# A seventh place for expert weights, and the expert blocks written out one by one

## The reference, cut to what matters

```python
def moe(h, w_router, b_router, w_gate, w_up, w_down):     # 16 experts, 2 for each token
    t = h.reshape(b * l, d)                               # d = 1024
    ... # scores, best group, the two best experts of it: gates (tokens x 16)
    hidden = jax.nn.silu(jnp.einsum('nd,edf->nef', t, w_gate)) * jnp.einsum('nd,edf->nef', t, w_up)
    out = jnp.einsum('nef,efd->nd', hidden * gates[..., None].astype(hidden.dtype), w_down)
```

## Time and profile before

| | |
|---|---|
| median of 3 runs | 1488.23 us (1484.03 to 1489.63) |
| the profiled execution | 1489.46 us |
| its span | 1487.5 us |
| TensorE busy | 1311.6 us, 88% of the span |
| VectorE, ScalarE, GpSimd busy | 525.2, 337.8, 163.6 us |
| expert layers | from about 582 to 865 us and from about 1202 to 1485 us |
| moved by DMA | 345.75 MB, of it 302.11 MB on SyncE's queue (q1) |

### The profile page before, as it was taken

How to read it: one execution, slowest core, us unless ns; L and a number is a source line. 1 busy time by engine, 2 the same in 40 slices (tenths; PEclk the granted TensorE clock), 3 DMA queues, 4 the chain that set the end, 5 groups by cost and what they waited for, 6 DMA issues and landing times.

```text
span 1487.5 us, 38763 instructions
## 1 busy us (share of the span) xinstructions
PE 1311.6 (88%) x16880; PEld 915.6 (62%) x16880; DVE 525.2 (35%) x1156; ACT 337.8 (23%) x671; POOL 163.6 (11%) x226
## 2 busy tenths in 40 slices
PE   5989999989999999999898669978899899988882
PEld 2448854468888547787676334545665578866651
DVE  1324444135456746111111053448455351111103
ACT  2223221142333123000000033433443220000001
POOL 2004310023343000000000030020000000000001
PEclk8999999999999998999999979978879899999996
DMA  9841157550111155999999881326314469999995
GB/s 398 310 164 60 60 195 237 174 205 9 54 60 60 58 203 221 356 387 391 397 405 418 362 318 57 113 73 226 114 57 170 175 230 378 400 395 394 392 426 193
DMA packets 39799, 345.75 MB, mean 232 GB/s; under 512 B 5611, under 2 KB 10555, under 8 KB 21360
## 3 DMA queue, kind: packets, MB, share of 16 engines
q1 hardware_dynamic: 21456, 302.11, 51.5%
q0 software_dynamic: 7104, 22.90, 4.7%
q10 hardware_dynamic: 11104, 18.75, 3.9%
HBM read 322.30 MB, written 21.45 MB: 231 GB/s over the span
## 4 chain that ended last, share of the span: by engine, by line
PE 65%; DMA 18%; issue 7%; DVE 6%; ACT 3%; ACTq 0%; DVEq 0%; POOLq 0%; POOL 0%; SPq 0%
PE PB L699 60%; DMA arena<-in_w_moe 15%; PE PB L702 6%; DVE arena L2037 3%; DMA ring<-in_w_mod 2%; ACT arena L1560 1%; DVE small L2050 1%; DMA expert_out<-arena 1%; DVE x L2037 1%; DVE arena L2044 0%; ACT hT L1560 0%; DMA arena<-expert_out,rows_i 0%; ACT L1560 0%; DVE arena L2047 0%; ACT ring L1560 0%
## 5 line engine op out<-in xcount | busy, mean ns | idle before, releaser
L699 PE MATMUL PB<-arena 64*64 64x64 f32 (+7 forms) x9524 | 477.1, 294 | 50.7 <-DMA arena<-in_w_moe 37.2
L699 PEld LDWEIGHTS PB<-arena 64*64 64x64 f32 (+3 forms) x9524 | 376.6, 130 | 146.2 <-issue 78.0
L699 PE MATMUL PB<-ring,hT 128*128 128x512 f32 (+1 forms) x720 | 314.0, 591 | 7.2 <-DVE hT L2040 3.6
L699 PEld LDWEIGHTS PB<-ring,hT 128*128 128x128 f32 x720 | 137.3, 194 | 167.2 <-issue 162.5
L699 PE MATMUL PB<-ring,arena 128*32 128x256 f32 (+2 forms) x3712 | 209.4, 380 | 9.9 <-DMA ring<-in_w_moe 7.0
L699 PEld LDWEIGHTS PB<-ring,arena 128*32 128x32 f32 x3712 | 172.4, 110 | 38.4 <-issue 9.9
L1560 ACT ACTIVATE arena<-PB 128x256 f32<-128x256 f32 (+3 forms) x217 | 106.4, 490 | 333.0 <-PE PB L699 279.5
L702 PE MATMUL PB<-cst,arena 128*128 128x128 f32 (+2 forms) x758 | 117.3, 296 | 42.5 <-ACT arena L1560 20.0
L702 PEld LDWEIGHTS PB<-cst,arena 128*128 128x128 f32 (+2 forms) x758 | 90.2, 155 | 88.1 <-issue 48.4
L2470 DVE TENSOR_TENSOR arena<-arena,PB 128x256 f32<-128x256 f32 (+1 forms) x32 | 15.1, 471 | 288.6 <-PE PB L699 168.5
L699 PE MATMUL PB<-ring,scT 128*32 128x512 f32 x384 | 60.8, 753 | 21.9 <-DMA ring<-in_w_mod 16.0
(11 more groups left out here) (148 smaller groups left out, 928.7 us busy)
## 6 DMA issues: line engine op xcount, KB each, us to landing
arena<-in_w_moe SPq DMA_DIRECT2D x50, 2048.0 KB, 24.5
ring<-in_w_moe SPq DMA_DIRECT2D x46, 2048.0 KB, 27.3
ring<-in_w_mod SPq DMA_DIRECT2D x24, 2048.0 KB, 8.5
ring<-in_w_mix SPq DMA_DIRECT2D x22, 2048.0 KB, 8.3
expert_out<-gate ACTq DMA_DIRECT2D x1, 3456.0 KB, 21.9
expert_out<-arena ACTq DMA_DIRECT2D x12, 288.0 KB
tokens<-arena ACTq DMA_DIRECT2D x6, 512.0 KB, 4.0
expert_out<-arena ACTq DMA_DIRECT2D x20, 128.0 KB
```

Of the source, the lines that this page charges most:

```text
L699: return nc.tensor.matmul(out, lhsT, rhs, start=start, stop=stop, **k)
```

## The change

Expert layers get a seventh place: 12 KB in each partition where the turned tokens `hT` stood and 4 KB where the mixer's gates stood (`gate[:, 2D:2D+1024]`). The up weights of blocks 2, 6, 10 and 14 go there, each as two transfers; those of blocks 4, 8 and 12 go to place 0 as before. The up load of block 2 waits for the last transpose of the turned tokens, and stands one row earlier in what it waits for: not the gate product of block 0, but the router. The up load of block 4 is issued right after the expert numbers are there. The up loads of the later even blocks wait for the up product of the block four before, not two before. Since the places now repeat every four blocks and not every two, the loops of TensorE and SyncE are gone: ten blocks are written out in their place. The loops of the other engines stay.

```diff
-        LOADS = (8, 9, 8, 8, 8, 7)
+        LOADS = (4, 9, 8, 8, 8, 7)
+        SPLIT = 6 * 512
+        seventh = [hT[:, 0:SPLIT], gate[:, 2 * D:2 * D + CHUNK - SPLIT]]
+        def up_loads(l, c):
+            return 4 * l + (c + 2) // 4 if c % 4 == 2 else 4 * l + 1 + c // 4
...
+            def even_up(L, l, c, e):
+                if c % 4 == 2:
+                    if c > 2:
+                        sp.wait_ge(*steps_of(L, "gu", None, c - 4))
+                    dram = io["w_moe"][l][1][bass.ds(e, 1)].rearrange("e p n -> (e p) n")
+                    sp.dma_start(seventh[0], dram[:, 0:SPLIT]).then_inc(sem("seventh_landed"), 16)
+                    sp.dma_start(seventh[1], dram[:, SPLIT:CHUNK]).then_inc(sem("seventh_landed"), 16)
+                else:
+                    sp.wait_ge(*steps_of(L, *(("ga", None, 0) if c == 4 else ("gu", None, c - 4))))
+                    weights(l, 1, e, 0, w_place[0])
...
                 early(l, 0, LEADERS[2], 5)
-                sp.wait_ge(*steps_of(L, "ga", None, 0))
-                early(l, 1, LEADERS[2], 0)
+                sp.wait_ge(*when("htok_p", l, TILES - 1, 1))
+                even_up(L, l, 2, LEADERS[2])
                 sp.wait_ge(*steps_of(L, "gu", None, 0))
                 early(l, 2, LEADERS[1], 1)
                 sp.wait_ge(*when("rows", l))
-                e3, e4 = expert(slice(3, 4)), expert(slice(4, 5))
-                gate_w(L, l, None, 3, 1, e3)
-                up_w(L, l, None, 3, 1, e3)
+                es = {c: expert(slice(c, c + 1)) for c in (3, 4)}
+                even_up(L, l, 4, es[4])
+                gate_w(L, l, None, 3, 1, es[3])
+                up_w(L, l, None, 3, 1, es[3])
                 down_w(L, l, None, 2, 0, LEADERS[2])
-                gate_w(L, l, None, 4, 0, e4)
-                with sp.Fori(1, half - 2) as i:
-                    es = [expert(bass.ds(i * 2 + n, 1)) for n in (1, 2, 3, 4)]
-                    for n in range(2):
-                        up_w(L, l, i, 2 + n, n, es[n + 1])
-                        down_w(L, l, i, 1 + n, 1 - n, es[n])
-                        gate_w(L, l, i, 3 + n, 1 - n, es[n + 2])
...
+                gate_w(L, l, None, 4, 0, es[4])
+                for c in range(3, NE):
+                    down_w(L, l, None, c, c % 2, es[c])
+                    if c + 2 < NE:
+                        es[c + 2] = expert(slice(c + 2, c + 3))
+                        gate_w(L, l, None, c + 2, c % 2, es[c + 2])
+                        if c % 2:
+                            up_w(L, l, None, c + 2, 1, es[c + 2])
+                        else:
+                            even_up(L, l, c + 2, es[c + 2])
...
+                    elif L in base_loop and m and c % 4 == 2:
+                        pe.wait_ge(sem("seventh_landed"), 32 * up_loads(l, c))
+                        w = [part[:, at:at + 512] for part in seventh for at in range(0, part.shape[1], 512)]
+                    elif L in base_loop and m and c % 4 == 0:
+                        pe.wait_ge(w_place[0], 16 * up_loads(l, c))
...
-                pair(None, [cap_of(n) for n in range(4)])
-                with pe.Fori(1, half - 2) as i:
-                    pair(i, (CAP, SMALL, CAP, SMALL))
-                pair(None, [cap_of(NE - 4 + n) for n in range(4)], NE - 4)
+                for c in range(1, NE - 1):
+                    rows_T(L, None, c + 1, (c + 1) % 2)
+                    down(L, None, c - 1, (c - 1) % 2, cap_of(c - 1))
+                    hidden_T(L, None, c, c % 2, cap_of(c), 1)
+                    gate_up(L, None, c + 1, (c + 1) % 2, cap_of(c + 1))
```

More of the change, by code:

```diff
@@ L1224, in gate_up @@
                         pe.wait_ge(*steps_of(L, "hid", i, c - L["k"]))
+                    l = L["base"] // NE
+                    w = wplace[(places or PLACE[b])[m]].rearrange("p (k n) -> p k n", k=KD)
+                    w = [w[:, k, :] for k in range(KD)]
                     if places:
-                        pe.wait_ge(w_place[places[m]], 16 * LOADS[places[m]] * (L["base"] // NE) + 16)
+                        pe.wait_ge(w_place[places[m]], 16 * LOADS[places[m]] * l + 16)
+                    elif L in base_loop and m and c % 4 == 2:
[3 more added lines that the diff above has]
+                        pe.wait_ge(w_place[0], 16 * up_loads(l, c))
                     else:
                         pe.wait_ge(*loads_of(L, L["land"][b][m], L["land_base"][b][m], i, c))
-                    w = wplace[(places or PLACE[b])[m]].rearrange("p (k n) -> p k n", k=KD)
                     for k in range(KD):
-                        ins = strips(2 + 2 * m + b, xT[:, b, CAP * k:CAP * k + cap], cap, w[:, k, :],
+                        ins = strips(2 + 2 * m + b, xT[:, b, CAP * k:CAP * k + cap], cap, w[k],
                                      slice(0, first), slice(first, FF), k == 0, k == KD - 1)
@@ L1272, in banks_free @@
                         reader[b] = None
[L1274 to L1281, removed]
                 banks_free(0, 1)
```

## The result

Of 20 runs each, the changed kernel's median is 1490.92 us (1486.99 to 1497.73), that of the kernel before 1484.39 us, from 1479.26 us up. One run of the kernel before took 2221.57 us and is left out of the ratio. The ratio is 1.0041, with a 95% interval from 1.0029 to 1.0054. The forecast was 1481.2 us, in a range of 1476 to 1488.5 us, with the same 0.48, faster 0.40 and slower 0.12. It was wrong in sign and the time lies outside the range, though the loss is within the 0.5% that the forecast counts as the same. The median of before had been 1488.23 us over three runs and was 1484.39 over twenty, so the reference of the forecast was 4 us high as well; against it the forecast gain of 7.0 us would have been 1477.4.

What follows compares the result with a forecast made beforehand. TensorE was taken to bound each expert layer early, the weight-load queue later; -4.9 + 0.3 + 1.1 = -3.5 us a layer, -7.0 us for two, gave 1481.2 us from a median of 1488.23, range 1476 to 1488.5.

Steps and rivals of the forecast that it cites:

- What bounds the kernel: Expert layers: TensorE sets the pace until about 685 us, afterwards the queue of weight loads, until load 48 lands.
- The seventh place: Start of each expert layer: nine loads instead of eight out before 600.8 us, so the last lands 4.9 us earlier.
- Does it turn dense at the same moment?: Weight stream from 585 to 603 us: cost of a later start, between 0 and 2.3 us a layer, taken as 0.3.
- Rival B: Start of the layer: the hole is filled but busy microseconds don't squeeze; 3.0 us less, 1485.2 us; chance 0.20.
- The gather: Block 2's gather beside one more load: rows may reach TensorE 1 to 2 us late, counted as no cost.
- Written out instead of looped: TensorE's ten blocks in a row: 15.7 more instruction packets a layer, costing 1.1 us a layer.
- the free branches: TensorE's loop: removing four backward branches gains nothing, since they cost nothing.
- even share: Instruction packets spread over 16 DMA engines: 15.7 x 1.1 / 16 = 1.1 us a layer.
- Rival C: Packets on one DMA engine hold back the weight stream, 1.1 us each: 25 us slower, 1513.6 us; chance 0.12.
- a constant 0.8 MB: Weight stream to 677.8 us: bytes moved beyond landed loads stay at 0.8 MB over three packets, so no single slow engine.
- The sum: Per expert layer -4.9 + 0.3 + 1.1 = -3.5 us; two layers -7.0 us.
- Each seventh load in two transfers: SyncE: 12 KB and 4 KB a partition, one issue more of 0.33 us, covered by SyncE's waiting.

Runs made afterwards that it cites:

- early: Kernel before, loops kept: only block 2's up weights use the seventh place, block 4's up load goes ahead of block 3's gate load; ratio 0.9986.
- unrolled: Kernel before with the middle blocks of TensorE and SyncE written out, six places and the old order of loads; ratio 1.0048.
- whole: Changed kernel with `hT` and `gate` side by side, so each load into the seventh place is one transfer; ratio to the kernel before 1.0015.

## Why the prediction was wrong

- **What bounds the kernel**: right. In all kernels the end of the layer followed the weight stream. A small misreading beside it: the DMA row has 8 in slice 23 and 5 in slice 40, not 9.
- **The seventh place, 4.9 us a layer if the stream turns dense at the same moment**: the loads went out where they were forecast; the "if" did not hold.
- **"Does it turn dense at the same moment? I take 0.3 us"**: failed. The term had bounds of 0 and 2.3 us, and I took the lower one, by the low GB/s of the gathers at a share near 1. The low GB/s was not room: I counted on 3.2 us of it, and 0.6 us were won back. The megabytes of `early` put the term at 4.9 - 2.5 = 2.4 us, about the upper bound. The landing of down 3 puts it at 4.9 - 3.8 = 1.1 us, its layers at 3.7 us with what is lost behind. Each of them is several times the 0.3 us, but the size stays uncertain. Rival B had the mechanism.
- **The gather, "I count none"**: TensorE waited 2.72 us in the changed kernel and 1.64 us in `early`. The DMA share behind it was 0.99 from 604 to 636 us, so the delay left no hole in the stream, and counting none was right.
- **"Written out instead of looped ... I take 1.1 us"**: failed, and this step decided the sign. The packets were counted well (139 against 138), the free branches were right, and the price was three times too low: 3.4 us a layer in `unrolled`, 0.2 us a packet, most of it by fewer bytes (0.13 us in that run, 0.17 by the averages) and the rest by drift between the engines. The timed runs say the same with a wide interval, 7.1 us (4 to 10) over 32 packets. My even share was 0.07 us.
- **Rival C**, the packets hold back the stream: it happened, at a fifth of the full price of 1.1 us that I gave it. I had set its threshold at 0.29 us a packet against a start worth 4.6 us a layer. With the start at the 1.2 us of `early`'s layers the threshold is 1.2 / 15.7 = 0.08 us, and 0.2 is far above it. B and C were priced as alternatives; both came, and only together do they make the sign. The test that I used against C (a constant 0.8 MB) covered three packets. The trace of the kernel before held a better one. From 600 us on (q1 and q8, first until 793.8 and then until 816 us, when 32 and 36 loads had landed):

```profile
q1 hardware_dynamic: 4652, 67.83, 88.7%
...
q8 instruction: 9, 0.15, 0.3%
...
q1 hardware_dynamic: 5263, 76.79, 89.3%
...
q8 instruction: 11, 0.18, 0.3%
```

Less 67.11 and 75.50 MB landed, the count is 0.7 MB after a long stretch without packets and 1.3 MB two packets later; at the end it is 1.2 MB. I had that stretch in the trace and didn't count it.
- **The sum**: forecast -4.9 + 0.3 + 1.1 = -3.5 us a layer. Measured by the parts: -1.2 (`early`) + 3.4 (`unrolled`) = +2.2 us; the changed kernel's layers are 2.5 us longer. By the timed runs the parts make -0.14% + 0.48% = +0.34%, against 0.41% measured. Both agree within the scatter, which is too wide to prove that the two parts simply add.
- **Each seventh load in two transfers**: counted as no loss. The layer lengths agree (+2.4 against +2.5 us, -1.1 against -1.2); the timed runs leave a small part of the loss open (1.0015 in `whole` against 1.0041).
- The Trainium skill (Runtime: NRT & Kernel Launch, "Instruction fetch mechanics") says that long straight code is streamed in 16 KiB blocks at a cost that is mostly hidden. The changed kernel agrees for TensorE: from 690 to 840 us every pause that its timeline lists ends with the landing of a weight load. It doesn't agree for the weight stream, which moved 0.9 MB less in `unrolled` than in the earlier trace rows while the DMA engines were full.

## What to carry to other kernels

Where the DMA engines are full, instruction fetches are traffic on the path: the loop whose body stayed loaded was free here, and writing it out cost about 0.2 us for every 16 KB of instructions. A transfer moved into an idle stretch is worth only what is also put in the place it leaves: count the bytes moved up to the moment when the queue is full for good, not the number of issues. And when two rivals are each priced against the full forecast gain, price them together too.

## What the runs showed of the hardware

- TensorE's loop of 264 products (some 65 KB of instructions by 246 bytes a product) was fetched once for five passes: no instruction packet from 664 to 798 us, and 16 there when the blocks were written out.
- An instruction packet of 16 KB holds one DMA engine for 1.1 us, which is 0.07 us over 16 engines; the weight stream lost 0.13 to 0.17 us of bytes for each, and 0.2 us with the drift (`unrolled` against before, and the averages of the windows from 664 to 798 us).
- Two gathers of 96 and 64 rows (0.66 MB) hold the DMA engines' share near 1 at 293 to 381 GB/s with weights beside them, for about 8 us (`early`, 591 to 599 us, shown below): 2.7 MB in place of the 3.4 MB that 428 GB/s would give. A share near 1 at a low rate was mostly not free room.

The windows of `early` behind that:

```profile
587.00:591.00 4.00, 3.67 (x33) 3.51 (x32) 0.47 (x2) 0.29 (x1) 1.89 (x2) 1.00 1.03 434
591.00:595.00 4.00, 3.65 (x66) 2.24 (x70) 0.69 (x2) 0.20 (x1) 0.00 (x0) 1.00 1.04 381
595.00:599.00 4.00, 3.80 (x72) 2.03 (x64) 0.08 (x1) 0.38 (x1) 0.00 (x0) 1.00 1.03 293
```
